# A fused transformer block: the first modulation in pieces of 256 columns, and the mixer's bias rows added on VectorE

## What is computed

```
mod = silu(c) @ ada_w[0] + ada_b[0]           # (6 * 1024 columns: sh1, sc1, g1, sh2, sc2, g2)
h   = rms_norm(x, norm_g[0, 0]) * (1 + sc1) + sh1
z   = gelu(h @ a_w_in)                        # 1024 x 2048
u, v = split(z);  v = layer_norm(v, a_ln_g, a_ln_b)
mixed = einsum('gts,bcsgd->bctgd', tril(a_w_s), v) + a_b_s
y   = (u * mixed) @ a_w_out
```

## Time and profile before

| | us |
|---|---|
| median of 3 runs | 1545.44 |
| lowest, highest | 1545.17, 1547.06 |
| the profiled execution | 1545.76 |
| its span (first to last instruction) | 1543.5 |
| PE, DVE, ACT, POOL busy in the span | 1503.5, 1068.7, 689.3, 275.2 |

### The profile page before, as it was taken

One profiled execution on the slowest core, in us unless ns is written; L12 is line 12 of the kernel. 1 busy time (PEld: TensorE's weight loads), 2 busy tenths in 40 slices (PEclk: granted clock), 3 DMA queues, 4 the chain that ended last, 5 costly groups with the idle time before them and its releaser, 6 DMA issues.

```text
span 1543.5 us, 20887 instructions
## 1 busy us (share of the span) xinstructions
PE 1503.5 (97%) x8203; PEld 1248.0 (81%) x8203; DVE 1068.7 (69%) x1588; ACT 689.3 (45%) x1200; POOL 275.2 (18%) x206
## 2 busy tenths in 40 slices
PE   4999999999999999989999999999999999999998
PEld 3888888888888897977778988888888888777777
DVE  6798688889989763258885785666634734588574
ACT  3433552322314454357774641323223544677771
POOL 0200013223232000059881011111100011100000
PEclk9999999999999999999999999999999999999999
DMA  9675256578585214330000254434423222112201
GB/s 331 245 259 191 82 192 239 186 249 307 190 274 190 92 51 142 105 115 2 2 1 29 82 208 165 144 120 141 164 82 109 86 87 78 55 60 75 77 8 55
DMA packets 108807, 203.33 MB, mean 132 GB/s; under 512 B 6042, under 2 KB 13479, under 8 KB 108711
## 3 DMA queue, kind: packets, MB, share of 16 engines
q1 hardware_dynamic: 108710, 202.01, 38.5%
HBM read 199.90 MB, written 2.10 MB: 131 GB/s over the span
## 4 chain that ended last, share of the span: by engine, by line
PE 81%; DVE 10%; ACT 2%; DMA 2%; issue 2%; SPq 1%; POOL 1%; DVEq 0%; ACTq 0%
PE PS L2245 46%; PE PS L2198 21%; DVE MACC L1327 3%; PE PS L2580 3%; PE PS L2607 2%; DVE WL L1293 2%; PE PS L2570 2%; PE PS L2510 1%; PE PS L2269 1%; POOL MROW L506 1%; DMA MRAW<-in_ada_w_dram 1%; DMA X<-in_x_dram 1%; DMA RAW<-in_ff_w_out_dram 1%; PE PS L2572 1%; DMA RAW<-in_ff_w_in_dram 1%
## 5 line engine op out<-in xcount | busy, mean ns | idle before, releaser
L730 ACT ACTIVATE WH<-RAW 128x2048 fp32r<-128x2048 f32 (+1 forms) x109 | 204.4, 1887 | 363.9 <-DMA RAW<-in_ff_w_in_dram 223.7
L1293 DVE TENSOR_TENSOR WL<-RAW,WH 128x2048 fp32r<-128x2048 f32 (+1 forms) x105 | 265.3, 2547 | 119.8 <-ACT WH L730 119.7
L506 POOL PARTITION_ALL_REDUCE MROW<-MACC x26 | 123.3, 4744 | 602.2 <-DVE MACC L1327 514.9
L2245 PE MATMUL PS<-WH,HIDh 128*128 128x512 f32 (+1 forms) x576 | 217.4, 377 | 0.0
L2245 PE MATMUL PS<-WH,HIDl 128*128 128x512 f32 (+1 forms) x576 | 217.3, 377 | 0.0
L2245 PE MATMUL PS<-WL,HIDh 128*128 128x512 f32 (+1 forms) x576 | 217.3, 377 | 0.0
L2245 PE MATMUL PS<-HTh,WH 128*128 128x512 f32 (+1 forms) x520 | 202.4, 389 | 0.4 <-DVE WL L1293 0.4
L2245 PE MATMUL PS<-HTl,WH 128*128 128x512 f32 (+1 forms) x520 | 202.4, 389 | 0.0
L2245 PE MATMUL PS<-HTh,WL 128*128 128x512 f32 (+1 forms) x520 | 202.3, 389 | 0.0
L1327 DVE SCALAR_TENSOR_TENSOR MACC<-MRAW,CS,MACC 128x512 f32<-128x512 f32 x168 | 126.3, 752 | 8.6 <-DMA MRAW<-in_ada_w_dram 1.1
L2245 PEld LDWEIGHTS PS<-WL,HIDh 128*128 128x128 f32 x576 | 108.3, 188 | 20.4
(11 more groups left out here) (351 smaller groups left out, 2998.1 us busy)
## 6 DMA issues: line engine op xcount, KB each, us to landing
MRAW<-in_ada_w_dram SPq DMA_DIRECT2D x44, 1024.0 KB, 7.4
RAW<-in_ff_w_in_dram SPq DMA_DIRECT2D x32, 1024.0 KB, 5.4
RAW<-in_ff_w_out_dram SPq DMA_DIRECT2D x32, 1024.0 KB, 5.1
RAW<-in_w_in_dram SPq DMA_DIRECT2D x16, 1024.0 KB, 5.2
MRAW<-in_w_ada_dram SPq DMA_DIRECT2D x12, 1024.0 KB, 8.8
RAW<-in_a_w_in_dram SPq DMA_DIRECT2D x8, 1024.0 KB, 9.9
MRAW<-in_kv_ada_w_dram SPq DMA_DIRECT2D x8, 1024.0 KB, 5.8
RAW<-in_kv_w_dram SPq DMA_DIRECT2D x6, 1024.0 KB, 5.3
```

Source lines behind the costliest of these rows:

```text
L506: pool.partition_all_reduce(MROW[:], MACC[:], P, RADD).then_inc(m_red, 1)
L730: act.activation(WH[:, wslot(u), 0:width(u)], RAW[:, u % 4, 0:width(u)], ACT.Copy).then_inc(w_hi, 1)
L1293: dve.tensor_tensor(WL[:, u % 4, 0:width(u)], RAW[:, u % 4, 0:width(u)], WH[:, wslot(u), 0:width(u)].bitcast(F32), ALU.subtract).then_inc( ...
L2245: mm = pe.matmul(po, a, b_, start=(k == 0 and i == 0), stop=(k == KT - 1 and i == len(ops) - 1), skip_group_check=len(ops) > 3)
```

## The change

What it does, part by part:

- The first two 512-column blocks of scale and shift are replaced by four passes i = 0 to 3. Pass i loads 256 columns of scale and 256 of shift (four DMAs of 512 KB, in PIECE buffers, `head_columns`), sums both into one accumulator (`head_acc`), where each instruction waits for the one before the last; TensorE sums over the partitions, and VectorE makes the coefficients of the blocks 2i and 2i + 1 (`head_coefs`). x is loaded behind pass 0. The half chunks of a_w_in come in quarters (two depths, `first_weight`), those for pass 0 among the tiles of x and the others behind the pieces of their pass.
- The order of the first two projections is by depth: both chunks take depth k before k + 1, in the order high x high for all banks, then the low parts (`depth`). The blocks 2 to 7 are turned one at a time into bank 3 (`turn_later`). The last bank of chunk 1 comes at the end as before. Three multiplications of IDENT with itself follow the transposes of each tile of x.
- ScalarE writes both HIDh and RB from PSUM; VectorE only subtracts (`remainder`). XR is gone.
- The small loads go partly to ScalarE's queue, partly behind the last pass. A root is taken ahead of the head.
- The turned a_w_s and the bias rows go through bank 3 in two halves each, one after the other. VectorE adds BS to MIXC, behind the sums of the fifth modulation; POOL's addition is gone.
- The gate rows of the sixth modulation are loaded behind the second half of chunk 2's weights.

```diff
@@ sync_program
+        def head_columns(i):
+            for h in range(2):
+                ks = slice(4 * h, 4 * h + 4)
+                if i >= 2:
+                    sp.wait_ge(h_acc, 16 * i - 24 + 8 * h)
+                for j in range(2):
+                    src = cols_of(ada[0], D * (1 - j) + 256 * i, 256)[:, ks, :]
+                    p = 2 * (i % 2) + j
+                    sp.dma_start(PIECE[p][:, ks, :], src).then_inc(h_in[i % 2][h], 16)
...
+        sp.dma_start(PR1[C_C:C_C + KT, :], c[0].rearrange("(r p) -> r p", p=P)).then_inc(c_in, 16)
+        head_columns(0)
+        for tt in range(TT):
+            if tt == 2:
+                first_weight(0, 0)
+            load_x(tt)
+        first_weight(1, 0)
+        for pair in range(1, 4):
+            head_columns(pair)
+            first_weight(0, pair)
+            first_weight(1, pair)
@@ pool_program
-        pool.wait_ge(mix_e, 2)
-        pool.wait_ge(bs_in, 16)
-        flat = lambda v: v.rearrange("p g t -> p (g t)")
-        pool.tensor_tensor(flat(MIXC[:]), flat(MIXC[:]), flat(BS[:]), ALU.add).then_inc(mix_cr, 1)
@@ act_program, head
-            for k in range(4):
-                act.wait_ge(full, 4 + k + 1)
-                scaled(k, PS[:, k, :], ev_a)
...
+            first_hi(0, 0)
+            for pair in range(4):
+                act.wait_ge(coef0, pair + 1)
+                scaled(2 * pair)
+                scaled(2 * pair + 1)
+                first_hi(1, pair)
+                if pair < 3:
+                    first_hi(0, pair + 1)
             for i in range(2):
-                act.activation(WST[:, 4 * i:4 * i + 4, :].rearrange("p g t -> p (g t)"), PS[:, i, :], ACT.Copy
+                act.wait_ge(mix_t, i + 1)
+                act.activation(WST[:, 4 * i:4 * i + 4, :].rearrange("p g t -> p (g t)"), PS[:, 3, :], ACT.Copy
                                ).then_inc(mix_w, 1)
-            hi(1)
-            act.wait_ge(mix_b, 1)
             for i in range(2):
-                act.activation(MIXC[:, 4 * i:4 * i + 4, :].rearrange("p g t -> p (g t)"), PS[:, 2 + i, :], ACT.Copy
+                act.wait_ge(mix_b, i + 1)
+                act.activation(MIXC[:, 4 * i:4 * i + 4, :].rearrange("p g t -> p (g t)"), PS[:, 3, :], ACT.Copy
                                ).then_inc(mix_e, 1)
@@ dve_program, head
+            def head_acc(i, half):
+                acc = (MACC, MROW)[i % 2]
+                for k in range(4 * half, 4 * half + 4):
+                    for j in range(2):
+                        a, p = acc[:, 256 * j:256 * j + 256], 2 * (i % 2) + j
+                        src = PIECE[p][:, k, :]
...
+                        else:
+                            dve.wait_ge(h_acc, 16 * i + 2 * k - 1 + j)
+                            dve.scalar_tensor_tensor(out=a, in0=src, scalar=CS[:, k:k + 1], in1=a,
+                                                     op0=ALU.mult, op1=ALU.add).then_inc(h_acc, 1)
...
+            first_lo(0, 0)
+            remainder(0)
+            head_acc(1, 0)
+            remainder(1)
+            first_lo(1, 0)
+            head_acc(1, 1)
+            first_lo(0, 1)
+            head_coefs(1)
+            for pair in range(1, 4):
+                if pair < 3:
+                    head_acc(pair + 1, 0)
+                remainder(2 * pair)
+                remainder(2 * pair + 1)
+                first_lo(1, pair)
...
@@ dve_program, behind the head
         for i in range(2):
             mod_acc(a_mods[i][0][0])
+            if i == 0:
+                dve.wait_ge(mix_e, 2)
+                dve.wait_ge(bs_in, 16)
+                flat = lambda v: v.rearrange("p g t -> p (g t)")
+                dve.tensor_tensor(flat(MIXC[:]), flat(MIXC[:]), flat(BS[:]), ALU.add).then_inc(mix_cr, 1)
             lo(4 + i)
             mod_post(*a_mods[i][0][1:])
@@ pe_program
+        for pair in range(4):
+            k = 2 * pair
+            if pair == 0:
+                depth(0, 0)
+            else:
+                depth(0, k, (lambda: turn_later(k + 1), None, None))
+            if pair < 3:
+                depth(0, k + 1)
+                depth(1, k)
+                head_columns(pair + 1)
+                depth(1, k + 1, (lambda: turn_later(k + 2), None, None))
+            else:
+                depth(0, k + 1, (None, lambda: weights_turned(0), None))
+                depth(1, k, (lambda: weights_turned(1), None, lambda: bias(0)))
+                depth(1, k + 1, (None, None, lambda: bias(1)))
+        pe.wait_ge(mix_e, 2)
```

More of the change, by code:

```diff
@@ L1417, in head @@
+            dve.wait_ge(ev_d, 2)
             normed(1)
[L1418 to L1420 removed]
+            head_coefs(0)
             normed(2)
@@ L2415, in pe_program @@
[L2415 to L2438 removed]
+            else:
+                pe.wait_ge(mix_e, 1)
```

389 lines of the change are left out of this document (184 added, 205 removed).

## The result

| us | kernel before | changed kernel |
|---|---|---|
| median of 17 runs | 1545.17 | 1547.82 |
| lowest, highest | 1543.73, 1547.06 | 1546.57, 1550.44 |
| the profiled execution | 1545.76 | 1548.73 |
| its span | 1543.5 | 1547.0 |

The ratio is 1.0017, with a 95% interval of 1.0011 to 1.0024: 2.65 us slower, just under the 0.2% that I had set as the line, and 0.7 us above my 1547.1. The range held it. The way the time came about is told by four views.

What follows compares the result with a forecast made beforehand. VectorE was taken as the bound from E to the MCOL copy, undoing TensorE's lead: +0.6 us there and +1.1 us for the lower level make +1.7 us on 1545.76, with the median 0.3 below: 1547.1 us, range 1542.0 to 1550.6.

Steps and rivals of the forecast that it cites:

- The first multiplication: Start of TensorE's first projection: at 22.2 us, 9.1 us earlier than before, given 21.4 to 23.7.
- The higher level at the start: Start of the projections: extra IDENT multiplications bring TensorE to its higher level by then, gaining 2.85 us.
- E: End of the last copy to MIXC, in the first two projections: forecast at 71.7 us.
- The sums: VectorE's 256-column sums in the head: 0.435 us apart, 6.7 us a pass, bounds 0.35 and 0.525.
- The third rival: Head: 256-column sums go 0.525 us apart, last MIXC copy at 75.2 us, time 1550.6 us; chance 0.12.
- From E to the sums of the sixth modulation: VectorE behind the last MIXC copy: 8.2 us, so the sixth modulation starts at 79.9 us, before 79.20.
- From there to the MCOL copy: VectorE from sixth modulation to MCOL: 29.2 - 1.5 + 2.4, done at 110.0 us, or 108.0 with short reduction.
- the length of GpSimd's reduction: Behind the fifth modulation's sums: 5.18 or 3.23 us, making VectorE wait 2.4 or 0.4 us.
- the lower level: TensorE after idling at mod_column(6) near 100 us: slower multiplications add 1.1 us, between 0.6 and 1.6.
- the next projection: Behind the first mixing stage: starts at 110.95 us, or 108.95, before 110.36; sign: 109 to 112 us.
- the eight slow multiplications of the earlier trace: Kernel before, 1357.79 to 1361.19 us, after a 2.16 us wait: 0.43 us apart, counted as 1.6 us lost.
- The second rival: From the last MIXC copy on: VectorE isn't late, the 6.9 us stay, time 1538.5 us; chance 0.08.

Runs made afterwards that it cites:

- e1: Changed kernel with the addition of BS to MIXC back on GpSimd, behind its reduction of the fifth modulation; 1550.66 us.
- e3: Changed kernel with 24 IDENT multiplications added on TensorE ahead of mod_column(6), to keep it busy in the wait; 1545.99 us.
- e6: Changed kernel without the twelve IDENT multiplications behind the transposes of x; 1549.01 us.
- e7: Changed kernel with each 256-column sum waiting for the instruction right before it, not the one before that; 1557.66 us.
- e4: Changed kernel with three quarters of the first mixing stage ahead of mod_column(6) and MCOL copied between chunk 3's two WL; 1546.35 us.
- e12: Changed kernel with the IDENT fill as 3, 3, 0 and 2 behind the four tiles of x, not 3 each; 1548.38 us.
- e5: Changed kernel with four moves: ScalarE's WH earlier, VectorE's list reordered, mod_column(6) behind three quarters of mixing, MCOL between the WL; 1539.51 us.
- e10: The e5 version with the IDENT fill as 3, 3, 0 and 2 behind the four tiles of x, not 3 each; 1539.14 us.
- e9: Kernel before with one change: VectorE, not GpSimd, adds BS to MIXC, behind the sums of the fifth modulation; 1544.89 us.
- e11: Changed kernel with only the ScalarE and VectorE moves of e5; mod_column(6) and the MCOL copy stay as in the changed kernel; 1543.51 us.
- e2: Changed kernel with ScalarE's WH of chunk 2 ahead of the MIXC copies and the BS addition behind the eighth modulation's sums; 1546.66 us.

## Why the prediction held, and where it was off

Point by point:

- **The first multiplication** was put at 22.2 us and came at 22.74. The loads were early (ScalarE begins with the first tile of x at 11.66 us, 12.4 predicted). What I left out is that the fill behind the third tile holds the turn of the fourth: V was ready at 20.02 us, the turn started at 21.30. It depends on when TensorE gets its level: in the profiled executions of e1 and e3, with the same head, the first multiplication was at 21.54 and 21.37 us.
- **The higher level at the start** is there from the first multiplication, but the 2.85 us that I counted for it are not in E: without the fill (e6) E is 1.0 us earlier than in the changed kernel's trace and 0.4 us later than in those where the level came early.
- **The sums**: 0.40 us apart, 0.435 predicted; the price of the full wait, 0.515, was predicted as 0.525. The third rival's mechanism is shown by e7; its size (1550.6 us) was far too small against 1557.7: it put E 3.5 us late and E came 8.7 us late, with TensorE at its lower level in two stretches, which the sum left out.
- **E**: 71.7 predicted, 73.12 in this execution; with the same head 71.86 us in e1, 71.67 in e3 and 72.93 in e4. The number was right for the executions in which the level comes early and up to 1.4 us short for the others.
- **From E to the sums of the sixth modulation**: 8.2 us predicted, 7.76 measured. **From there to the MCOL copy**: 30.1 predicted, 29.97 measured. I had left the length of GpSimd's reduction open as chance; it is none (below), and the long one was certain here.
- **The step that failed in size is the lower level.** It was put at 1.1 us, bounded by 0.6 and 1.6. It was 2.6 us in this execution (e3), and 1.7 and 1.8 us in those of e6 and e12. With it the next projection started at 114.6 us, outside the 109 to 112 us that I had named as a sign. I had sized it by the eight slow multiplications of the earlier trace rows and called those 1.6 us lost; even there the loss is only 0.85 us, since the traces without them wait for VectorE a little later instead (in the changed kernel at 1364.57 us). Here the level stayed low for the whole stage, 1.04 us in mod_column (1.83 against 0.79) and 2.63 us in the mixing stage (6.31 against 3.68), and of the 3.7 us together the wait for MCOL, which goes with them, would have taken 1.1 us anyway.
- **What brought the sum back near 1547.1**: E and the level made the next projection 4.46 us late and not 0.6 + 1.1, which is 2.8 us too little. Against it stand 0.96 us behind that place, 0.5 us around the span, which I had held fixed, and 0.6 us because this execution lies 0.9 us above its median, where I had taken 0.3. That the error is only 0.7 us is luck to that extent: the path and its bound were right, and 2 us of errors cancelled.
- **The second rival** (the 6.9 us stay, 1538.5 us) is close to what e5 and e10 show when VectorE's order is mended: 1539.5 and 1539.1 us. I had called VectorE the bound from E on, which was right for the change as it is.

## What to carry to other kernels

When a start gets faster, follow the first wait behind it to the engine that ends it, and look at the order of that engine's list: TensorE's 5 us of lead were lost because VectorE and ScalarE waited ahead of work that could have gone first, and a change of order on three engines gave them back. Price an idle stretch of TensorE by its length plus the lower level behind it, over all the work of that stage, and shift independent work into it; halving it moved the next stage by 4.2 us and the time by only 1.9 us (e4). A wait two instructions back lets short instructions follow closely (0.40 against 0.515 us), and is worth more than its own time where TensorE waits for the result (e7).

## What the runs showed of the hardware that I had not expected

**The length of GpSimd's reduction is set by VectorE.** Up to 500 us the fourteen traces hold 280 of these reductions. In 195 VectorE had begun a WL (RAW and WH from SBUF, 2.29 us) 0.2 us ahead of them, and every one of these took 5.17 to 5.21 us. Of the other 85, 84 took 3.23 to 3.25 us; at their start VectorE stood still, did statistics or read PSUM. The last one, in e9, started 0.2 us behind the addition of 1.22 us and took 4.11 us. e5 has both lengths:

```profile
70.33 5.18 POOL L509 PARTITION_ALL_REDUCE MROW<-MACC  x1 [20.77 <-DVE MACC L1343]
83.04 3.23 POOL L509 PARTITION_ALL_REDUCE MROW<-MACC  x1 [7.53 <-DVE MACC L1343]
```

The first follows WL at 70.11 us, the second the statistics at 82.85 us. The other way round, the addition of 1.22 us took 2.96 us in e5 beside a running reduction, and WL 4.33 us in e9. The Trainium skill, SBUF — State Buffer, section Who interferes with whom, says that a VectorE instruction with two inputs in SBUF contends with a GpSimd one that reads SBUF. It calls the ports that the two share an exclusive lock, and says, of VectorE's modes that use two ports, that whoever issues first has them for the whole instruction and the other is fully blocked. That the two contend agrees with the traces. The full block agrees where the reduction comes second: it is 1.95 us longer, and WL had 2.07 us to go. It doesn't where VectorE comes second. In e5 the reduction ended at 75.51 us; fully blocked, the addition would have ended at 76.7 us, and it ended at 75.58. In e9 the reduction ended at 73.09 us; fully blocked, WL would have ended at 75.4 us, and it ended at 74.23.

**TensorE's level falls after short waits, and not in every execution.** Waits of 1.69 us (e11), 3.24 us (e4), 4.91 us (e2) and 6.01 us were followed by a granted clock of 0.50 to 0.79. Far behind the change all fourteen traces have a wait of 2.16 to 2.19 us near 1360 us. In five (the kernel before, e2, e4, e11, e12) it is followed by six to eight slow multiplications, in the other nine it is not; from this wait to the next one of over 1.3 us it is 36.64 to 36.69 us in the five and 35.78 to 35.84 us in the nine, so that the slow multiplications cost 0.85 us. The same is seen near 680 us: e6 loses 2 us there and the changed kernel nothing. So executions can differ by 0.85 us at the one place and 2 us at the other through this alone, and a lead of 1 us in one trace (e12) says little about the medians.
